# Routed experts in pairs: the order of matmuls inside a pair, and one transfer per expert and panel

## The reference, cut to what matters

```python
for each token: two of 64 experts, with gates            # router
hid = silu(xb @ w_gate[e]) * (xb @ w_up[e])              # (1024 -> 512) twice
y   = hid @ w_down[e]                                    # (512 -> 1024)
out = rmsnorm(h + sum over its two experts of gate * y)
```

## Time and profile before

| | |
|---|---|
| median of 3 runs | 1533.67 us (1533.14 to 1534.39) |
| the profiled execution's own time | 1533.78 us |
| its span, first to last instruction | 1531.8 us |
| granted TensorE clock, mean | 0.988 of 2.4 GHz |
| PE busy | 1452.1 us, 95% of the span |
| DVE, ACT, POOL busy | 565.3, 455.0, 69.9 us |
| transfers | 491.84 MB |
| chain that ended last | PE 67%, DMA 23%, DVE 4% |
| first and last record of the expert blocks | 636.5 and 1520.8 us |

### The profile page before, as it was taken

The page is one execution under the profiler, slowest core; times in us unless marked ns, Lnnn a source line. Parts: engine busy times, 40 slices in busy tenths (PEclk is TensorE's granted clock), DMA queues, the critical chain, the costliest instruction groups (busy, mean ns, idle before and its releaser), DMA issues.

```text
span 1531.8 us, 20132 instructions
## 1 busy us (share of the span) xinstructions
PE 1452.1 (95%) x7657; PEld 879.1 (57%) x7657; DVE 565.3 (37%) x869; ACT 455.0 (30%) x773; POOL 69.9 (5%) x62
## 2 busy tenths in 40 slices
PE   7999999999999999999999988988988989999997
PEld 6888988888889877543444333332432433444342
DVE  5865877753677968411111111110110111111112
ACT  5634655533565674311111111110110111111112
POOL 1000000000020082100000000000000000000000
PEclk9999999999999999999999999999999999999999
DMA  9564346454554446999999999999999999999996
GB/s 329 172 219 165 138 159 214 171 205 153 192 165 166 111 138 214 415 420 419 414 423 422 422 422 422 422 421 423 422 422 422 422 421 422 423 421 417 423 421 252
DMA packets 110133, 491.84 MB, mean 321 GB/s; under 512 B 9655, under 2 KB 15931, under 8 KB 63484
## 3 DMA queue, kind: packets, MB, share of 16 engines
q1 hardware_dynamic: 108364, 484.43, 79.8%
q0 software_dynamic: 1504, 6.37, 1.3%
q10 hardware_dynamic: 208, 0.28, 0.1%
HBM read 508.82 MB, written 1.10 MB: 333 GB/s over the span
## 4 chain that ended last, share of the span: by engine, by line
PE 67%; DMA 23%; DVE 4%; POOL 2%; issue 2%; ACT 1%; SPq 1%; DVEq 0%; ACTq 0%; POOLq 0%
DMA slots<-in_w_up_dram 22%; PE banks L1648 20%; PE banks L1124 20%; PE banks L1683 8%; PE banks L1191 7%; PE banks L1192 3%; PE banks L1590 3%; PE banks L1600 2%; POOL areas L615 1%; DVE w_split L1788 1%; POOL areas L614 1%; SPq L497 1%; PE banks L1114 1%; DVE areas L2091 0%; ACT w_split L700 0%
## 5 line engine op out<-in xcount | busy, mean ns | idle before, releaser
L1648 PE MATMUL banks<-slots,xeT 128*64 128x512 f32 x1536 | 353.4, 614 | 40.5 <-DMA slots<-in_w_up_dram 40.5
L1648 PEld LDWEIGHTS banks<-slots,xeT 128*64 128x64 f32 x1536 | 111.8, 141 | 277.0 <-issue 213.8
L1683 PE MATMUL banks<-slots,heT 128*64 128x512 f32 x1024 | 226.8, 595 | 8.0 <-ACT heT L1043 8.0
L1788 DVE TENSOR_TENSOR w_split<-raw,w_split 128x2048 fp32r<-128x2048 f32 (+1 forms) x96 | 206.0, 2171 | 76.5 <-ACT w_split L700 76.4
L700 ACT ACTIVATE w_split<-raw 128x2048 fp32r<-128x2048 f32 (+1 forms) x95 | 168.4, 1806 | 59.5 <-PE banks L1124 54.5
L2367 DVE TENSOR_TENSOR h_e<-banks,h_e 128x512 f32<-128x512 f32 x32 | 22.1, 692 | 420.9 <-PE banks L1648 420.9
L1191 PE MATMUL banks<-h_both,w_split 128*128 128x512 f32 x448 | 158.2, 398 | 0.0
L1683 PEld LDWEIGHTS banks<-slots,heT 128*64 128x64 f32 x1024 | 70.7, 137 | 145.2 <-issue 131.1
L1124 PE MATMUL banks<-w_split,h_both 128*128 128x512 f32 (+1 forms) x624 | 143.1, 385 | 2.4 <-DVE h_both L1778 2.3
L2379 DVE SCALAR_TENSOR_TENSOR y_lo<-banks,stats,y_hi 128x512 fp32r<-128x512 f32 x63 | 44.4, 746 | 230.3 <-ACT y_hi L1057 230.3
L1124 PEld LDWEIGHTS banks<-w_split,h_both 128*128 128x128 f32 x624 | 112.1, 188 | 26.8 <-issue 3.8
(11 more groups left out here) (355 smaller groups left out, 1422.7 us busy)
## 6 DMA issues: line engine op xcount, KB each, us to landing
slots<-in_w_up_dram SPq DMA_DIRECT2D x126, 1024.0 KB
slots<-in_w_down_dram SPq DMA_DIRECT2D x126, 1024.0 KB
areas<-in_w_gate_dram SPq DMA_DIRECT2D x64, 1024.0 KB, 17.7
slots<-in_w_gate_dram SPq DMA_DIRECT2D x64, 1024.0 KB
raw<-in_w_in_dram SPq DMA_DIRECT2D x38, 1024.0 KB, 5.4
raw<-in_w_ff_dram SPq DMA_DIRECT2D x32, 1024.0 KB, 5.3
raw<-in_w_out_dram SPq DMA_DIRECT2D x8, 1024.0 KB, 5.1
raw<-in_w_in_dram SPq DMA_DIRECT2D x10, 512.0 KB, 4.0
```

What stands on the lines that cost most here:

```text
L1648: last = mm(bank[SLOTS * e:SLOTS * e + SLOTS, :], xeT[:, k, odd, SLOTS * e:SLOTS * e + SLOTS], expert_panel(w, e, odd)[:, k, :], start=(k ...
L1683: last = mm(banks[half][SLOTS * e:SLOTS * e + SLOTS, :], heT[:, c, SLOTS * e:SLOTS * e + SLOTS], expert_panel("down", e, odd)[:, c, 512 * ...
L1788: last = tt(lo, source, hi, ALU.subtract)
```

## The change

In the gate and up blocks the loops over e and k change places: all eight k of expert 0 come first, then all eight of expert 1. In the down block expert 0 does both of its output halves before expert 1 begins. A wait stands before each expert's run for that expert's panel alone, and the count is raised after each expert's run. SP loads a whole panel with one transfer of 2 MB (16 KB in each partition) once the same expert's last use has been counted. Semaphore thresholds go from 32 to 16 per pair accordingly. In the last pair expert 1's up and down panels come in two halves, and PE waits for the second at k = 4 and before c = 2. All other engines' programs stay as they are, and so does the number of matmuls and of bytes.

```diff
 # load (SP)
-                rows = 2 if w == "down" else 4
-                for piece in range(3 if closing else 2):
-                    half = min(piece, 1)
+                every_row = 4 if w == "down" else 8
+                for e in range(2):
                     if not isinstance(i, int) or (w == "gate" and i > 1) or (w != "gate" and i > 0):
-                        sp.wait_ge(used, 2 * i - (3 if w == "gate" else 1) + half)
-                    part = slice(rows * half, rows * half + rows)
...
-                    for e in range(2):
+                        sp.wait_ge(used, 2 * i - (3 if w == "gate" else 1) + e)
...
+                    at_once = every_row // 2 if closing and e else every_row
+                    for start in range(0, every_row, at_once):
+                        part = slice(start, start + at_once)
+                        landed_now = last_landed[w] if start else pair_landed["odd_gate" if w == "gate" and odd else w, e]
                         cond = {} if beyond is None else {"cond": tokens[e] > beyond}
                         sp.dma_start(expert_panel(w, e, odd)[:, part, :],
 # experts (PE)
-                    for k in range(KT):
-                        if k % 4 == 0 and w == "gate":
-                            pe.wait_ge(pair_landed["odd_gate" if odd else w, k // 4], 32 * (couple + 1))
-                        elif k % 4 == 0:
-                            pe.wait_ge(pair_landed[w, k // 4], 32 * (i + 1))
-                        if k == 6 and w == "up" and odd and last_one:
-                            pe.wait_ge(last_landed[w], 2 * (couple + 1))
-                        for e in range(2):
+                    for e in range(2):
+                        if w == "gate":
+                            pe.wait_ge(pair_landed["odd_gate" if odd else w, e], 16 * (couple + 1))
+                        else:
+                            pe.wait_ge(pair_landed[w, e], 16 * (i + 1))
+                        for k in range(KT):
+                            if k == 4 and e and w == "up" and odd and last_one:
+                                pe.wait_ge(last_landed[w], couple + 1)
                             last = mm(bank[SLOTS * e:SLOTS * e + SLOTS, :], xeT[:, k, odd, SLOTS * e:SLOTS * e + SLOTS],
                                       expert_panel(w, e, odd)[:, k, :], start=(k == 0), stop=(k == KT - 1))
-                        if k % 4 == 3:
-                            last.then_inc(done, 1)
+                        last.then_inc(done, 1)
...
-                for half in range(2):
-                    down(0, half)
-                down(1, 0)
-                down(1, 1).then_inc(downed, 1)
-                pe.wait_ge(pair_landed["down", 1], 32 * (i + 1))
+                pe.wait_ge(pair_landed["down", 0], 16 * (i + 1))
+                down(0, 0, 0, 1, 2, 3)
+                down(0, 1, 0, 1, 2, 3).then_inc(downed, 1)
+                pe.wait_ge(pair_landed["down", 1], 16 * (i + 1))
                 if odd and last_one:
                     for half in range(2):
-                        down(2, half)
-                    pe.wait_ge(last_landed["down"], 2 * (couple + 1))
-                    down(3, 0).then_inc(half_downed, PAIRS // 2)
-                    down(3, 1).then_inc(downed, 1)
+                        down(1, half, 0, 1)
+                    pe.wait_ge(last_landed["down"], couple + 1)
+                    down(1, 0, 2, 3).then_inc(half_downed, PAIRS // 2)
+                    down(1, 1, 2, 3).then_inc(downed, 1)
                 else:
-                    for half in range(2):
-                        down(2, half)
-                    down(3, 0)
-                    down(3, 1).then_inc(downed, 1)
+                    down(1, 0, 0, 1, 2, 3)
+                    down(1, 1, 0, 1, 2, 3).then_inc(downed, 1)
```

More of the change, by code:

```diff
@@ L291, in program @@
             sem("t_made"), sem("t_rounded"), sem("t_ready"), sem("routed"), sem("route_max"), sem("route_exp"), sem("marks_ready"), sem("ranks_made"), sem("marks_done"))
-        pair_landed = {(w, half): sem(f"{w}_{half}_landed") for w in ("gate", "odd_gate", "up", "down")
-                       for half in range(2)}
+        pair_landed = {(w, e): sem(f"{w}_{e}_landed") for w in ("gate", "odd_gate", "up", "down")
+                       for e in range(2)}
         picked, gathered, xe_a, xe_d = sem("picked"), sem("gathered"), sem("xe_by_scalar"), sem("xe_by_vector")
@@ L476, in load @@
                 tokens = [None if beyond is None else tokens_of(pair, e) for e in range(2)]
-                rows = 2 if w == "down" else 4
-                for piece in range(3 if closing else 2):
-                    half = min(piece, 1)
+                every_row = 4 if w == "down" else 8
+                for e in range(2):
                     if not isinstance(i, int) or (w == "gate" and i > 1) or (w != "gate" and i > 0):
-                        sp.wait_ge(used, 2 * i - (3 if w == "gate" else 1) + half)
-                    part = slice(rows * half, rows * half + rows)
-                    if closing and half:
-                        part = slice(rows * (piece + 1) // 2, rows * (piece + 2) // 2)
-                    landed_now = last_landed[w] if piece == 2 else pair_landed["odd_gate" if w == "gate" and odd else w, half]
-                    for e in range(2):
[L487 to L495, removed]
@@ new lines, in load @@
+                        sp.wait_ge(used, 2 * i - (3 if w == "gate" else 1) + e)
+                    if isinstance(i, int) and (w, i) == ("gate", 0):
+                        sp.wait_ge(turned, turns_before(T_SSD) + 4)
+                        sp.wait_ge(mean_ready, 7)
+                    elif isinstance(i, int) and (w, i, e) == ("up", 0, 0):
+                        sp.wait_ge(w_ready, 2 * NP)
+                    elif isinstance(i, int) and (w, i, e) in (("up", 0, 1), ("down", 0, 0)):
+                        sp.wait_ge(half_projected, 2)
+                    elif isinstance(i, int) and (w, i) in (("down", 0), ("gate", 1)):
+                        sp.wait_ge(half_projected, 4)
@@ L1679, in experts, with down @@
                     pe.wait_ge(xe_d, 2 * couple + 4)
-                pe.wait_ge(pair_landed["down", 0], 32 * (i + 1))
-                def down(c, half):
-                    for e in range(2):
+                def down(e, half, *chunks):
+                    for c in chunks:
                         last = mm(banks[half][SLOTS * e:SLOTS * e + SLOTS, :], heT[:, c, SLOTS * e:SLOTS * e + SLOTS],
```

## The result

The changed kernel takes 1871.13 us (median of 4 runs, 1868.85 to 1872.34), the kernel before in the same series 1533.47 us (4 runs, 1533.14 to 1534.39). The ratio is 1.2192, 95% interval 1.2175 to 1.2209. The profiled execution took 1872.17 us. One execution of the twelve of the last experiment took 2105.84 us at a granted clock of 0.653 and is left out of its comparison.

The account below looks back on a forecast made before the run. PE bounds the expert stage at start and end, transfers its middle. 1533.8 + 463.3 (lost overlap) - 59.5 (waits gone) - 0.9 (end) = 1936.7 us; range 1915 to 2145.

Parts of the forecast that it names:

- What bounds the kernel: Expert stage: PE sets the pace at start and end, transfers in the middle; waiting and lowered clock worth 59.5 us.
- Alternating puts two records in an interval: Expert blocks: experts 0 and 1 stream simultaneously in their array halves, 32 records in 16 intervals of 0.429 us.
- About four places for each half: PE's queue: some 30 instructions behind the wait point, about four places per half beyond it; sets when expert 1 starts.
- L = 13: Lag between starts of two experts' runs: 13 intervals, three overlapped; 67.7 us per interval if off; forecast's chance 0.62.
- L = 12: Rival: expert 1 starts earlier, from more places beyond the wait point; 1869 us, each further place pair 68 less; chance 0.04.
- program order: Rival: PE's matmuls keep the program's sequence, only loads pulled ahead; 2072 us at lag 15, 2004 at 14, 2140 at 16; chance 0.22.
- The three terms of the sum: Added PE time: 30 down-gate-up sections 432.0 us, two two-block sections 20.0, two lone blocks 11.2; stated total 463.3.
- The end: Last scatter: ACT's and DVE's copies move ahead of PE's end, so the scatter no longer waits for them; -0.9 us.
- The 16 KB rows: 2 MB panel transfers: same rate assumed, no gain; at half the rate some 19 us more per pair.
- Side by side: Rival: PE looks past all 30 waiting instructions of expert 0, both halves overlap; 1534 to 1541 us; chance 0.05.
- the other side: Rival: halves overlap and 2 MB transfers also shrink the middle window's waits; 1474 to 1531 us; chance 0.03.
- the lower clock: Rival: half-filled array granted 1.2 GHz instead of 2.4 in part or all of the stage; up to 3036 us; chance 0.04.

Follow-up runs that it names:

- the last experiment: Kernel before, with only the gate panels in one 2 MB transfer per expert, awaited and given back whole: 1534.31 us (median of 11 runs), ratio 1.0001.
- the order alone: Changed kernel's PE order with the transfers and waits of the kernel before (1 MB halves): 1868.4 us.
- half width: Changed kernel with 256 moving columns per matmul instead of 512, in twice as many matmuls: 2010.24 us.
- runs of two: Kernel before, but PE takes two matmuls of expert 0, then two of expert 1, and so on: 1535.17 us (10 runs), ratio 1.001.

## Why the prediction was wrong in size and right in kind

**What bounds the kernel.** Right. The 59.5 us of waits and lower clock are exactly what the sections of before hold above 20.23 us, and they are gone.

**Alternating puts two records in an interval.** Right: the order alone makes the whole loss, and in the changed kernel 16 passes of one half last 16 intervals, overlapped only at the handovers.

**"About four places for each half": the step that failed.** The prediction stated L = 13 and the trace has 12. It read 34 stored instructions out of the earlier trace rows and split them into a queue of some 30 and four places per half. Nothing in the rows of before shows that split: with neighbours alternating, any number from three up would give the same block. The earlier trace rows show only that three are passed, and the stall in the earlier trace rows only that fewer than 32 fit before the point where waits are checked. Five was as good a reading as four. The runs show that one half's next run starts when five instructions of the other still wait, in runs of 16, 8 and 4 passes and at half width. So there are five places, or six if the load that starts at the same moment still has one; the runs don't part these. The price was stated right, 67.7 us per interval: 1936.7 - 67.7 = 1869.0, and 1872.17 was measured.

That these are places of each half is a reading, and not shown. A single window at the head of one queue, in which five or six waiting instructions may be passed whichever half they belong to, gives the same lag in every run above, since at each handover only the one half has instructions waiting ahead of the other's new run. The stored counts lean to places of each half: when the sequencer steps out of a down block, 33 instructions are stored at half width (1097.3, 48 loads and 47 matmuls of 128 begun), where expert 1's half runs alone, and 36 in runs of two (1083.77, 15 loads and 13 matmuls of 64), where both run. No run was made to part the two.

**The bounds of that step.** Here the range went wrong. The row supported "three or more" on one side, and the argument against more places, that the stalled queue held back at 32 instructions, says nothing of what lies beyond the wait point. L = 12 deserved a chance like that of 13 and not 0.04, and its 1869 belonged inside the range. The rival named the right mechanism and the right time; what was wrong is the chance that it got. The range instead reached to the rival of program order, on the side where no row spoke for it.

**The terms.** The three terms of the sum add up to 463.2 us, not 463.3, which changes nothing. Forecast against measured, per section: 14.40 against 12.29 us; for two blocks 10.0 against 8.7; for a lone block 5.6 against 5.2. With 12 in place of 13 the section's formula gives 5 x 12 + 15 - 47 = 28 intervals, 12.01 us, and 0.25 for five starts: 12.26. The starts at 0.05 us were right. The end, -0.9, and the clock, 1.00, were right. The rate, forecast at 313 GB/s, was 302 over the stage; in a couple's window it is 328 (25.2 MB in 76.4 us). The forecast rate was that of a couple; over the stage 302 GB/s x 1222.5 us are 369 MB of the experts' 403. The packets in the trace are those of 183 panels and not 192: three experts have no tokens and are skipped (19 MB), so that some couples load only 19 MB, and some 15 MB land before the stage begins. The same holds before the change.

**The wait ahead of expert 1's run**, priced at 0: confirmed by the run without it.

**The 16 KB rows**, taken at the same rate with no gain: in the changed kernel right, since PE hides them. With PE alternating they bring about 1% more rate (427 GB/s against the 422 that every alternating version with 1 MB transfers alone has in the middle window), and the steps that come with them cost more: 0.8% of the time. The Trainium skill ("SBUF — State Buffer", "The DMA setup-cost knee") says, for transfers that set the pace, to coalesce into the largest single transfer one can. From 1 to 2 MB this case gains that 1% in rate and nothing in time.

**The rivals.** Program order (2004 to 2140) fell: the matmuls of three passes of expert 0 are still to come when expert 1's first starts, and the lag is 5.21 us and not 6.4. The rule in the Trainium skill ("TensorE: Matmul & The Clock Gate", Part 2), that matmuls stay in program order and only weight loads are pulled ahead, therefore does not hold here between the two column halves of the array. Side by side and the other side fell with the couple of 76.4 us, the lower clock with the 1.00 of the stage.

## What to carry to other kernels

Two narrow matmuls that use different column halves run at once only if the program alternates between them closely: changing every four passes costs 0.1% here (interval 0 to 0.2%), every eight 2.5%, every sixteen 22%. When a number is read out of a store that two parts share, write down which splits of it the rows allow, and let the range take in each of them. Splitting the steps of waiting and giving back was worth more than longer transfers; for the panels with two places neither showed in the time.

## What was unexpected in the hardware

Matmuls of one column half start ahead of earlier ones of the other half, as soon as no more than five instructions of that other half wait (six with the load that starts at the same moment). The limit is counted in instructions and not in time (lag 5.21 us at 0.43 us per pass, 6.1 us at 0.22). A matmul of one half passes up to three matmuls of the other that the program has ahead of it. Some 33 to 36 instructions are stored in all when the sequencer steps out of a block, 33 with one half alone and 34 to 36 with both. A half that stood idle takes 0.48 us for its first pass instead of 0.43 and keeps that offset of 0.05 us.
